# Hybrid RG-LRU and convolution trunk on one core: order of the first loads, and low halves of the normalised tiles on VectorE

## What is computed

```python
h = concat([meta, x])                       # 528 tokens
hn = rms_norm(h, norm_g)
xa, sa, vb, gb, sb, ma, mb = split(hn @ w_in)      # 7 x 2048 columns
ya = rg_lru(causal_conv4(xa), ...) * silu(sa)       # gates: 16 heads of 128 x 128
yb = silu(layer_norm(causal_conv31(vb * sigmoid(gb)))) * silu(sb)
merged = sigmoid(ma) * (ya @ w_proj_a) + sigmoid(mb) * (yb @ w_proj_b)
out = rms_norm(h + merged @ w_out, final_g)[16:]
```

## Time and profile before

| | us |
|---|---|
| median of 3 runs | 1760.83 |
| lowest, highest run | 1760.11, 1762.89 |
| the profiled execution, its own time | 1761.53 |
| its span in the profile | 1759.7 |

### The profile page before, as it was taken

How to read it: one execution, slowest core, us unless ns; L and a number is a source line. 1 busy time by engine, 2 the same in 40 slices (tenths; PEclk the granted TensorE clock), 3 DMA queues, 4 the chain that set the end, 5 groups by cost and what they waited for, 6 DMA issues and landing times.

```text
span 1759.7 us, 26383 instructions
## 1 busy us (share of the span) xinstructions
PE 1740.8 (99%) x10796; PEld 1572.1 (89%) x10796; DVE 1315.6 (75%) x1562; ACT 868.9 (49%) x1106; POOL 297.2 (17%) x330
## 2 busy tenths in 40 slices
PE   9899999999999999999999999999999999999998
PEld 8899999999999988888888888888788888888886
DVE  7969888888888888788878878898633288775431
ACT  6556556565565523555555555556422254443322
POOL 0502213112122100111211112221100111120000
PEclk9999999999999999999999999999999999999999
DMA  6247768667686564877765767685667579857422
GB/s 209 89 124 161 185 162 180 144 152 180 163 175 145 145 190 140 208 215 221 211 164 162 200 180 197 184 216 153 239 219 243 173 209 207 198 170 237 146 82 96
DMA packets 285385, 311.02 MB, mean 177 GB/s; under 512 B 9425, under 2 KB 239953, under 8 KB 284113
## 3 DMA queue, kind: packets, MB, share of 16 engines
q1 hardware_dynamic: 211024, 188.21, 33.8%
q0 software_dynamic: 74240, 121.13, 31.8%
HBM read 235.38 MB, written 44.56 MB: 159 GB/s over the span
## 4 chain that ended last, share of the span: by engine, by line
PE 93%; DVE 4%; ACT 1%; issue 1%; DMA 0%; SPq 0%; DVEq 0%; ACTq 0%
PE psum L904 28%; PE psum L803 25%; PE psum L764 17%; PE psum L807 13%; PE psum L996 7%; PE psum L1010 3%; PE psum L871 1%; DVE t_parts L1843 0%; DVE region L1944 0%; DVE x_parts L1718 0%; DVE region L1557 0%; ACT x_parts L1045 0%; DVE w_lo L1718 0%; DMA region<-in_x_channels 0%; DVE region L1736 0%
## 5 line engine op out<-in xcount | busy, mean ns | idle before, releaser
L1240 ACT ACTIVATE w_hi<-raw 128x1024 fp32r<-128x1024 f32 x110 | 116.2, 1057 | 282.5 <-PE psum L764 135.8
L1491 DVE SCALAR_TENSOR_TENSOR region<-region,params 128x512 f32<-128x512 f32 x368 | 250.7, 747 | 0.0
L1711 DVE TENSOR_TENSOR w_lo<-raw,w_hi 128x1024 fp32r<-128x1024 f32 x110 | 134.9, 1227 | 128.1 <-ACT w_hi L1240 128.1
L904 PE MATMUL psum<-x_parts,w_hi 128*128 128x264 f32 x1792 | 227.1, 284 | 0.0
L904 PEld LDWEIGHTS psum<-x_parts,w_hi 128*128 128x128 f32 x1792 | 222.0, 188 | 0.0
L1718 DVE TENSOR_TENSOR w_lo<-region,w_hi 128x1024 fp32r<-128x1024 f32 x108 | 131.9, 1223 | 69.0 <-ACT w_hi L1256 68.8
L1718 DVE TENSOR_TENSOR x_parts<-region,x_parts 128x1024 fp32r<-128x1024 f32 x108 | 131.9, 1223 | 56.4 <-ACT x_parts L1256 56.2
L904 PE MATMUL psum<-x_parts,t_parts 128*128 128x264 f32 x1344 | 167.9, 284 | 0.0
L904 PEld LDWEIGHTS psum<-x_parts,t_parts 128*128 128x128 f32 x1344 | 165.2, 188 | 0.0
L803 PE MATMUL psum<-t_parts,w_hi 128*128 128x512 f32 x576 | 144.8, 393 | 0.2 <-ACT aux L1294 0.2
L803 PE MATMUL psum<-t_parts,x_parts 128*128 128x512 f32 x576 | 144.4, 393 | 0.0
(11 more groups left out here) (224 smaller groups left out, 3100.5 us busy)
## 6 DMA issues: line engine op xcount, KB each, us to landing
raw<-in_w_in SPq DMA_DIRECT2D x112, 512.0 KB, 4.0
region<-in_w_in SPq DMA_DIRECT2D x56, 1024.0 KB, 6.1
wide<-region POOLq DMA_DIRECT2D x98, 256.0 KB, 4.8
region<-in_w_proj_b SPq DMA_DIRECT2D x16, 1024.0 KB, 8.6
raw<-in_w_out SPq DMA_DIRECT2D x32, 512.0 KB, 3.8
raw<-in_w_proj_a SPq DMA_DIRECT2D x31, 512.0 KB, 3.9
region<-in_w_in POOLq DMA_DIRECT2D x28, 512.0 KB, 7.9
sigmoid_spill<-wide POOLq DMA_DIRECT2D x16, 512.0 KB, 3.3
```

Source lines behind the costliest of these rows:

```text
L904: last = pe.matmul(psum[:, bank + h, 0:HALF], weights[:, k // 2, (k % 2) * P:(k % 2 + 1) * P], part[:, KH * half + k, h * HALF:(h + 1) * H ...
L1240: act.activation(cut_at(n)[0], raw_at(n).rearrange("p (k n) -> p k n", k=4), ACT.Copy).then_inc(hi_ready, 1)
L1491: ins = dve.scalar_tensor_tensor(conv_b[:, t, :], moved, w, conv_b[:, t, :], ALU.mult, ALU.add)
L1711: dve.tensor_tensor(lo, raw_at(n).rearrange("p (k n) -> p k n", k=4), hi.bitcast(F32), ALU.subtract).then_inc(lo_ready, 1)
```

## The change

- SP issues the first loads in a new order and in smaller pieces (`first_loads`): meta tokens, x tile 0, parameters, half of chunk 0, x tile 1, the other half, x tiles 2 and 3, chunk 1, x tiles 4 to 7. x tiles 12 to 15 come in one load.
- PE works on chunk 0 by halves of the tokens (`first_chunk`): first the half without meta tokens. ACT cuts chunk 0 in two parts, and makes x tile 1 between them.
- All low halves of the normalised tiles are made by DVE; POOL has no arithmetic left in the first body.
- ACT makes the first tap of the xa convolution (`begin_conv_a`) in the first body too.
- In ACT's and DVE's programs several steps of chunks 8 to 11 change places.
- At the switch to w_proj_a, chunks 0, 1 and 2 are issued ahead of the four loads of ya; chunk 2 waits for the low half of the last S3 instead of that of chunk 0.

```diff
@@ SP @@
                 for p, source in enumerate(sources):
+                    if p < 2:
+                        continue
                     if x_too and p < 4:
-                        for n in (2 * p, 2 * p + 1) if p else (0,):
-                            sp.dma_start(channels[:, 2 * n:2 * n + 2, :], x_channels[:, 2 * n:2 * n + 2, :])\
-                                .then_inc(x_loaded[n], 16)
+                        for n in (4, 5) if p == 2 else (6,):
+                            tiles = slice(2 * n, 2 * n + 2 if n < 6 else CT)
+                            sp.dma_start(channels[:, tiles, :], x_channels[:, tiles, :]).then_inc(x_loaded[n], 16)
...
+            def first_loads():
+                sp.dma_start(meta_x, meta_channels).then_inc(meta_loaded, 16)
+                sp.dma_start(channels[:, 0, :], x_channels[:, 0, :]).then_inc(first_x_loaded[0], 16)
+                sp.dma_start(params[:, :, :], parameters).then_inc(params_loaded, 16)
+                w = w_in_v[:, 0:4, COL_XA:COL_XA + 256]
+                sp.dma_start(raw_v[:, 0, 0:2, :], w[:, 0:2]).then_inc(first_w_loaded, 16)
+                sp.dma_start(channels[:, 1, :], x_channels[:, 1, :]).then_inc(first_x_loaded[1], 16)
+                sp.dma_start(raw_v[:, 0, 2:4, :], w[:, 2:4]).then_inc(raw_loaded[0], 16)
+                for n in range(1, 4):
+                    sp.dma_start(channels[:, 2 * n:2 * n + 2, :],
+                                 x_channels[:, 2 * n:2 * n + 2, :]).then_inc(x_loaded[n], 16)
+                    if n == 1:
+                        sp.dma_start(raw_v[:, 1], w_in_v[:, 4:8, COL_XA:COL_XA + 256]).then_inc(raw_loaded[1], 16)
...
+                elif n == A0 + 2:
+                    sp.wait_ge(lo_ready, chunk(NX - 1, S3) + 1)
...
-            load_pa(0)
-            load_ya(0)
-            load_pa(1)
-            load_ya(1)
-            load_ya(2)
-            load_ya(3)
-            for m in range(2, 4 * PAIRS):
+            for m in range(3):
+                load_pa(m)
+            for n in range(4):
+                load_ya(n)
+            for m in range(3, 4 * PAIRS):
@@ POOL @@
-            for j in range(LO_BY_DVE, CT):
-                pool.wait_ge(norm_hi, j + 1)
-                pool.tensor_tensor(x_lo[:, j, META:T], channels[:, j, :], x_hi[:, j, META:T].bitcast(F32),
-                                   ALU.subtract).then_inc(norm_lo_pool, 1)
@@ PE @@
+            def first_chunk():
+                hi, lo = cut_at(0)
+                def passes(weights, parts, h):
+                    for k in range(4):
+                        if weights is hi and h:
+                            if k != 1 and k != 3:
+                                pe.wait_ge(first_hi_ready if k == 0 else hi_ready, 1)
+                            pe.wait_ge(raw_x_lo, k + 1)
+                        for m in range(2):
+                            for part in parts:
+                                last = pe.matmul(psum[:, 2 * m + h, 0:HALF], weights[:, k, m * P:(m + 1) * P],
+                                                 part[:, k, h * HALF:(h + 1) * HALF], ...)
+                    return last
+                passes(hi, (x_hi, x_lo), 1)
+                pe.wait_ge(meta_lo, 1)
+                passes(hi, (x_hi, x_lo), 0)
+                pe.wait_ge(lo_ready, 1)
+                passes(lo, (x_hi,), 1)
+                passes(lo, (x_hi,), 0).then_inc(multiplied, 1)
...
-                pe.wait_ge(meta_lo, 1)
-                for g in range(4):
+                first_chunk()
+                for g in range(1, 4):
...
-                    pe.wait_ge(norm_lo, min(4 * g + 4, LO_BY_DVE))
-                    wait(pe, norm_lo_pool, 4 * g + 4 - LO_BY_DVE)
+                    pe.wait_ge(norm_lo, 4 * g + 4)
@@ ACT, first_body @@
-                raw_tiles(range(0, 2))
+                raw_tiles(range(0, 1))
                 act.wait_ge(meta_normed, 1)
                 act.activation(x_hi[:, :, 0:META], meta_x, ACT.Copy).then_inc(meta_hi, 1)
-                cut_hi(0, 0)
+                act.wait_ge(first_w_loaded, 16)
+                act.activation(hi[:, 0:2, :], raw_v[:, 0, 0:2, :], ACT.Copy).then_inc(first_hi_ready, 1)
+                raw_tiles(range(1, 2))
+                act.wait_ge(raw_loaded[0], 16)
+                act.activation(hi[:, 2:4, :], raw_v[:, 0, 2:4, :], ACT.Copy).then_inc(hi_ready, 1)
                 raw_tiles(range(2, 8))
...
                 cut_gates_hi(0)
+                for t in range(2):
+                    act.wait_ge(norm_lo, t + 4)
+                    begin_conv_a(0, t)
                 cut_c_hi(0, 0)
                 cut_hi(0, 8)
                 norm_tiles_hi(8)
                 cut_c_hi(0, 1)
-                cut_hi(0, 9)
-                act.wait_ge(norm_lo_pool, 7 - LO_BY_DVE)
+                norm_tiles_hi(9)
+                act.wait_ge(norm_lo, 7)
                 read_gates(0, 0)
                 cut_c_hi(0, 2)
-                norm_tiles_hi(9)
+                cut_hi(0, 9)
+                read_gates(0, 1)
+                norm_tiles_hi(10)
                 cut_hi(0, 10)
-                read_gates(0, 1)
+                cut_c_hi(0, 3)
                 for t in range(2):
                     act.wait_ge(ma_scaled, t + 1)
                     act.activation(first_ma[:, t, :], psum[:, 4 + t, :], ACT.Sigmoid).then_inc(first_ma_gated, 1)
-                norm_tiles_hi(10)
-                cut_c_hi(0, 3)
                 cut_hi(0, 11)
@@ DVE, first_body @@
                     for j in range(4 * p, 4 * p + 4):
+                        if j == 2:
+                            dve.wait_ge(meta_hi, 1)
+                            dve.tensor_tensor(x_lo[:, :, 0:META], meta_x, ...).then_inc(meta_lo, 1)
...
                 cut_lo(0, 7)
-                dve.wait_ge(norm_lo_pool, 1)
-                conv_a_taps(0, range(KA), (0,), conv)
+                conv_a_taps(0, range(1, KA), (0,), conv)
                 cut_gates_lo(0)
                 cut_c_lo(0, 0)
                 norm_tiles(8)
                 cut_lo(0, 8)
                 cut_c_lo(0, 1)
-                dve.wait_ge(norm_lo_pool, 2)
-                conv_a_taps(0, range(KA), (1,), conv)
+                conv_a_taps(0, range(1, KA), (1,), conv)
+                norm_tiles(9)
+                cut_c_lo(0, 2)
                 cut_lo(0, 9)
-                norm_tiles(9)
-
+                norm_tiles(10)
+                cut_lo(0, 10)
+                cut_c_lo(0, 3)
                 group_done(0, 8)
                 for t in range(2):
                     dve.tensor_tensor(psum[:, 4 + t, :], psum[:, 4 + t, :], total[:, :], ALU.mult)\
                         .then_inc(ma_scaled, 1)
-                cut_c_lo(0, 2)
-                cut_lo(0, 10)
-                norm_tiles(10)
-                cut_c_lo(0, 3)
                 cut_lo(0, 11)
...
                 for j in NORM_TILES[p]:
                     dve.scalar_tensor_tensor(channels[:, j, :], ...).then_inc(x_normed, 1)
-                    if 1 <= j <= LO_BY_DVE:
+                    if j > NORM_TILES[p][0]:
                         tile_lo(j - 1)
+                tile_lo(NORM_TILES[p][-1])
```

More of the change, by code:

```diff
@@ L220, in hybrid_trunk @@
         params_loaded, meta_loaded = sem("params_loaded"), sem("meta_loaded")
-        x_loaded = [sem(f"x_loaded{n}") for n in range(PAIRS)]
+        first_x_loaded, first_w_loaded = [sem(f"first_x_loaded{j}") for j in range(2)], sem("first_w_loaded")
+        first_hi_ready = sem("first_hi_ready")
+        x_loaded = {n: sem(f"x_loaded{n}") for n in range(1, PAIRS - 1)}
         x_reloaded = [sem(f"x_reloaded{t}") for t in range(TT)]
@@ L270, in hybrid_trunk @@
         p_ready = sem("p_ready")
-        merged_summed = [sem(f"merged_summed{s}") for s in range(2)]
         merged_loaded = [sem(f"merged_loaded{g}") for g in range(PAIRS)]
@@ L873, in gate_round @@
                 last.then_inc(gates_multiplied, 1)
+            def first_chunk():
[9 more added lines that the diff above has]
+                                last = pe.matmul(psum[:, 2 * m + h, 0:HALF], weights[:, k, m * P:(m + 1) * P],
+                                                 part[:, k, h * HALF:(h + 1) * HALF],
+                                                 start=k == 0 and weights is hi and part is x_hi, stop=False)
+                    return last
[5 more added lines that the diff above has]
+                passes(lo, (x_hi,), 0).then_inc(multiplied, 1)
             def first_body():
-                pe.wait_ge(meta_lo, 1)
-                for g in range(4):
+                first_chunk()
+                for g in range(1, 4):
                     multiply(0, g, all_tokens(((0, 1), (2, 3))), g, raw_x=True)
@@ L1117, in first_body @@
                 act.activation(stats[:, 0:CT], stats[:, 0:CT], ACT.Exp, scale=-1.0).then_inc(lambda_exp, 1)
-                act.wait_ge(norm_lo_pool, CT - LO_BY_DVE)
+                act.wait_ge(norm_lo, CT)
                 branch_end(0)
@@ L1149, in xa_copy, with begin_conv_a @@
```

(29 more changed lines are left out.)

20 lines of the change are left out of this document (8 added, 12 removed).

## The result

| | us |
|---|---|
| median of 10 runs after | 1765.13 (1763.93 to 1769.35) |
| median of 10 runs before, beside them | 1760.14 (1759.59 to 1762.89) |
| ratio, 95% interval | 1.0026 (1.0018 to 1.0035) |
| the profiled execution, its own time and its span | 1765.73, 1763.9 |

The change makes the kernel 0.26% slower, 5.0 us. From one profiled execution to the other the span grows by 4.2 us, from 1759.7.

What follows compares the result with a forecast made beforehand. The matmul engine bounds the kernel, busy 1740.8 of 1759.7 us. Start +2.5, first body +4.6, switch -3.7 give +3.4, taken as +3.8 for the high ends: 1764.6 us against the median 1760.83, 8-in-10 range 1760.5 to 1768.5.

Steps and rivals of the forecast that it cites:

- Start: First loads and chunk 0: later x tiles delay ACT's cut of chunk 1, +1.5 us, plus slow clock +1.0.
- The second part: Start: a 2 us stall ahead of chunk 1 also costs clock, 0 to 1.7 us, taken as +1.0.
- First body: ACT's moved gate reads stall PE's second gate round 7.7 us; +2.4 us in order, +2.2 in clock.
- the clock, +2.2: First body: low clock behind the long stall costs at least 1.6, up to 3.4 us; 2.2 taken.
- DVE's own work about balances: First body: DVE's 7.8 us for GpSimd's low halves is covered by 4 to 9 us coming back.
- the cover: First body: without GpSimd beside it, DVE's taps run faster, 0.9 us for three; 4 to 9 us back.
- Switch: Switch to w_proj_a: chunks 1 and 2 load before ya, so PE's stall and its slow clock go; 3.74 us gained.
- The stall term, 2.04: Switch: PE's wait of 2.04 us goes, as ACT's chain can start up to 2.75 us earlier.
- The 1.70 of clock: Switch: the 16 matmuls behind the stall take 3.79 us instead of 5.49.
- rival 1: Faster: the moved reads do not bind, so first-body stalls of 6.5 us go; 1752 us, chance 0.07.
- rival 2: No visible change: last x pair lands near 11.5 to 12.3, or chunk 1's stall costs no clock; about 1762.6 us, chance 0.32.
- rival 3: Clearly slower: switch gives only 0 to 2 us, or low clock lasts through both long stalls; 1768.3 us, chance 0.15.

Runs made afterwards that it cites:

- chunk1_last: The changed kernel with chunk 1's weights loaded behind x tiles 6 and 7 instead of behind x tiles 2 and 3; 1764.55 us.
- best2: The changed kernel with the old start and, in the first body, ACT's gate reads and cuts of chunks 9, 10 ahead of tiles 8 to 11's high halves; 1752.74 us.
- reads_first: The changed kernel with ACT cutting chunk 9 and reading the first gate round ahead of the high halves of tiles 8 to 11; 1759.89 us.
- warm_fill28: The changed kernel with 28 dummy PE products filling the stall ahead of the second gate round; 1764.05 us.
- dve_lows_only: The kernel before with GpSimd's 13 low halves made by DVE, every order of steps as before; 1758.55 us.
- switch_only: The kernel before with only the new order of loads at the switch to w_proj_a; 1758.01 us.
- switch_undone: The changed kernel with the loads at the switch in their old order; 1768.24 us.
- start_only: The kernel before with the new start alone: first loads, chunk 0 by token halves, first cuts of ACT and DVE; 1761.87 us.
- best2_newstart: The changed kernel, its new start kept, with ScalarE's and VectorE's first-body order taken from best2; 1754.64 us.

## Why the prediction was right

The forecast was 1764.6 us, slower by 0.2% with a chance of 0.50; it is 1765.13 and slower. By its steps:

- **Start, +2.5 (0 to +4.2).** Measured +1.9 in the trace and 1.6, 1.7 and 1.9 in three pairs of medians. The cut of ACT was forecast at 16.5 and came at 16.86. The load named was the wrong one: I had x tiles 6 and 7 hold ACT at 13.1, and tiles 4 and 5 held it at 12.25, with four tiles to make behind them, which comes to nearly the same. Tiles 6 and 7 landed at 5.64 + 7.9 = 13.5, just as ACT reached them. The second part, +1.0 for a slow clock behind a 2 us stall, failed. I had chunk 0 end at 15.6; in that trace it ended at 17.7, because the pieces waited 0.66 and 1.43 us for their x tiles and the last 24 products of its high half ran for the most part at the 1.2 GHz level (granted clock 0.50 from 12 to 14). So the stall ahead of chunk 1 was 0.23 and not 2, and chunk 1 itself took 6.12 as before. The slow clock did come, inside chunk 0, where it was hidden behind ACT's late cut. In the three traces where it did not come, the stall ahead of chunk 1 was 1.52 to 1.53 us and no clock was lost behind it, so the +1.0 has no trace on its side. Whether the pieces of 256 KB land late, as the prediction estimated beside its sum, the runs don't settle: the last of chunk 0 landed at 8.1 in the changed kernel and at 7.5 in chunk1_last, with the same pieces, against 7.7 before and 8.5 in best2, with whole loads.
- **First body, +4.6 (+2.4 to +6).** Measured +6.4 in the trace. The mechanism is the one forecast, and reads_first and best2 show it: 7.7 us of stall ahead of the second gate round were forecast and 7.32 came (the round starts at 71.3 on the old axis, against 71.0), and of the wait ahead of chunk 9 1.61 came for 1.5. The term that was mis-sized is the clock, +2.2. From 73.25, the start of the round, it took 3.28 us to chunk 9 instead of 2.2 (the round's products took 0.42 us instead of 0.28), and from there to its low half 83.23 - 76.53 = 6.70 instead of 3.9: 3.9 us in all where I had taken 2.2, and above my upper end of 3.4. In the medians, total less start and switch gives +5.0 - 1.6 + 2.2 to 3.1 = +5.6 to +6.5, so the term seems too low there as well, by 1 to 2 us. Against that stands the 1.1 us that warm_fill28 gives back, and in the trace the clock was the dearest of four executions; the runs don't settle how much of the medians' +6 is clock.
- **The low halves' balance.** "DVE's own work about balances" holds: 2.37 us for the taps, VectorE's busy total 1313.9 against 1315.6 in dve_lows_only, and a gain of 1.6 us. What I called the cover was there.
- **Switch, -3.7 (0 to -3.74).** In the trace -4.2, but -2.2 (switch_only) and -3.1 (switch_undone) in medians. The stall term, 2.04, is about right (1.71 to 2.04 in the four traces that have the stall). The 1.70 of clock were read from one execution and do not come in every one: start_only, dve_lows_only (3.91 us for the same 16 matmuls) and switch_undone have the stall without them.
- **Sum.** In the trace the first body was 1.8 dearer, the start 0.6 and the switch 0.5 cheaper than forecast: +3.4 became +4.1. In the medians the start cost 0.6 to 0.9 less than forecast, the first body 1.0 to 1.9 more, and the switch gave 0.6 to 1.5 less. The direction and the main step follow from the mechanism; that the time came within 0.5 us of the forecast is in part luck, as errors of both signs met, and 0.4 us had been added to the sum for its high ends.

The rivals: rival 1, that the moved reads do not bind, is refuted by the 7.32 us. It is the order and not the engine that stood between the change and rival 1's time: with reads, cuts and low halves ahead of the tiles, best2_newstart reaches 1754.6, near the 1752 given there. Of rival 2's two conditions the first did not come true: the last x pair landed at 13.5 and not by 12.3. The second, a stall ahead of chunk 1 that costs no clock, did in three traces, and the start cost 1.6 to 1.9, a little over its +1.5; it was the dearer first body and the smaller gain at the switch that took the time out of its reach. Of rival 3 the half on the clock came true in the trace, where the low level lasts through both waits of the first body; but the switch gave more than 2, and the time stayed 3.2 us below its 1768.3.

## What to carry to other kernels

When work moves from one engine to another, look at what else in the hand-written order moves with it: a read of 0.5 us placed behind work that waits for a third engine cost 7.3 us, and two swapped lines gave 5.2 back. What frees the bound engine (here reads of PSUM and cuts of the next weights) goes ahead of what only fills buffers for later. Before a load is brought forward, list what else its consumer engine must do first: chunk 1's weights came early, but the cut stood behind x tiles that came late.

## What the runs showed of the hardware

- Stalls of nearly the same length are followed by slow clock or not. At the switch, stalls of 2.04 and 1.86 us (the second in dve_lows_only) were followed by 5.49 and 3.91 us for the same 16 matmuls. Behind 1.52 to 1.53 us of idle time 48 products took 6.11 to 6.12 us, as at the 2.4 GHz level, in three traces; behind 3.26 to 3.27 us ahead of the third gate round they took 7.29, 7.62 and 8.03 (start_only, before, switch_only). After 7.3 us of idle time the level was low in all four traces that had it, and it stayed low into the next busy stretch, for 3 us of chunk 9 (switch_undone) up to 6 (the changed kernel).
- Dummy products during a stall held the granted clock at 1.00 in the profiled execution (6.41 us of them, then 1.05 us idle).
- Splitting the first loads brought the first product forward by 1.8 us (9.35 to 7.54), and the kernel won nothing by it. With chunk 1's weights behind x tiles 2 and 3, tiles 4 and 5 let ACT go on only at 12.25; with the same pieces and the weights behind tiles 6 and 7 (chunk1_last) ACT had them all without a wait from 8.79.
